# Asking for three weight matrices sooner, and moving the routing's small tables out of two weight cells

## The chip, the cores and the metric

The kernel runs on one core of one Trainium2 chip. The metric is the device time of a whole run in microseconds (us), median of several runs; the profile is of one execution, and its times count from the start of its span.

## The reference

One decoder layer on 256 tokens of width 1024, all in float32. A mixer (three head groups: stick-breaking attention, a gated linear recurrence, cross attention) is normalised by groups, projected and added to x. Then comes the mixture of experts, which is where nearly all bytes are:

```python
scores = sigmoid(t @ w_router)                    # 256 x 64
choice = scores + router_bias
# best 4 of 8 groups of experts by the sum of their two best choices, then top 8 experts in those
_, eidx = top_k(where(emask, choice, -inf), 8)
w = scores at eidx, divided by their sum, times 2.5
for each of 64 experts e (w_gate, w_up: 1024 x 256, w_down: 256 x 1024):
    out += gate[:, e] * ((silu(t @ w_gate) * (t @ w_up)) @ w_down)
out += one shared expert of the same shape, for every token
```

The weights of one expert are 3 MiB, those of all 64 are 192 MiB, and the shared expert has 3 MiB more.

## The kernel before

**Stages.** TensorE (PE) works through a list of units of the mixer (semaphore `unit_ps` counts them), then twelve pieces of the output projection (`projections`, counted by `wo_ps`; pieces 1 to 4 read rows k = 0 to 3 of the matrix `wo`, pieces with k = 4, 5 come as 5, 6, 9, 10, those with k = 6, 7 as 7, 8, 11, 12), the transposes of the normalised x1 into `xn2T`, the router's product (`rt_ps`), the counts, and then 28 groups of experts.

**Groups.** Experts 1 to 6 of the list are fixed (the reference's first six). The other 58 are ranked by how many tokens chose them, and their ids are known only when the vector engine writes `ids` (`ids_dve`). A group holds one, two or four experts side by side in 128 columns; two groups (8 and 15) are halves of the shared expert, which stands in the list as expert 0. For each group PE gathers its tokens, does gate and up with the weights' low half and high half (`gu_ps` goes up after each), the down product (`y_ps`, two steps), and the scatter into four accumulators.

**Cells.** Weights go into 22 cells of 8 KB per partition (1 MiB each) and one more that is used once. A matrix part is "low" or "high" (halves of gate and up) or "down"; each is 1 MiB. From group 8 on "low" and "high" of an expert may come as one load of 2 MiB ("both") into two neighbouring cells, and from group 16 on all three parts as one of 3 MiB ("whole") if three neighbours are free soon enough. A planner at build time (`take`, `last_use`, `held`, `used_at`) walks the list of loads and gives each the cells whose present contents are used up first. Two cells have special places: cell 15 at `o_O + 8 KB` and cell 21 at `o_O + 16 KB`. Before the change the routing's small tensors (`w_rt`, `rbias`, `top8`, `gtop`, `grep`, `score`, `choice` in the first, `cand`, `repl`, `gatew`, `pos_T` in the second) lie in them, so that low 7 (cell 15) waits for `gates_dve`, and cell 21 is held by an entry ("late", None) until `gateT_ps` and `gates_dve`.

**The order of loads.** All weight loads are issued by the sync engine (SP) on one queue, in program order; SP waits in front of a load until its cell is free, and everything behind it waits too. The order of the first ones is written by hand (lines 528 to 564); from line 566 on it is the planner's list: down 0, low 7, low 8, low 9, low 10, high 7, and so on. Down 0 waits for the last step of `split_dve` (the low part of x1, made by the vector engine at L1239) and for `residual_ps`, since it lands on x1. A ranked load also waits for `ids_dve` and reads its expert's id into a register (L571).

Names in the rows: `cell_gu` is a 1 MiB gate/up load, `cell_d` a down load, `cell_two` and `cell_three` those of 2 and 3 MiB. L473 issues them all. L1641 are the projections, L1564 the column sums of `y_sq`, L1676 the router's product, L1734 the gather, L1776 gate and up, L1805 down, L1834 the scatter.

Of the kernel before, what the change touches and what calls it, by code (L numbers as in the profile page):

```python
# [5 lines left out]
def hybrid_decoder_layer(  # L6
# [12 lines left out]
    ACT = mybir.ActivationFunctionType  # L19
    AX = mybir.AxisListType  # L20

    P = 128
    _, SEQ, D = x.shape
    NT = SEQ // P
    KD = D // P
# [3 lines left out]
    NE, GROUPS, DE = w_router.shape[2], 8, w_down_sh.shape[1]  # L29
# [8 lines left out]
    CELLS = 22  # L38
# [15 lines left out]
    for i, kind in enumerate(kinds):  # L54
# [9 lines left out]
        if kind != "fixed":  # L64
            r = {"single": singles, "pair": pairs, "quad": quads}[kind].pop(0)
# [12 lines left out]
    loads, used_at = [], {}  # L78
# [22 lines left out]
    def at(name, offset, shape, dt=F32):  # L101
        return nc.alloc_sbuf_tensor_at(name, shape, dt, offset=offset)
# [23 lines left out]
    neighbours = [(a, b) for a in range(CELLS) for b in range(CELLS) if cell_at[b] == cell_at[a] + 8 * KB]  # L126
    held = dict(zip(first_cells, loads))
    del held[CELLS]
    held[CELLS - 1] = ("late", None)
    used_at["late", None] = (0, 1.5)  # L130
    fills = [1] * (CELLS - 1) + [0, 1]
    cell_of = dict(zip(loads, first_cells))
    landed = {load: (i, 1) for load, i in cell_of.items()}
# [77 lines left out]
    rg_t = r("rg_t", [P, 2, SEQ])  # L211
    rg_u = r("rg_u", [P, 2, SEQ])
    y_sq = at("y_sq", o_R + 16 * KB, [P, KD, SEQ])
    x1_sq = at("x1_sq", o_R + 8 * KB, [P, D])
    xhi = at("xhi", o_R, [P, NT, KD, P], F32R)
    xn2T = at("xn2T", o_R + 16 * KB, [P, KD, SEQ])
    yhi = at("yhi", o_R + 16 * KB, [P, D], F32R)
    ylo = at("ylo", o_R + 20 * KB, [P, D], F32R)

# [26 lines left out]
    rstd_row = at("rstd_row", r.offset + 7 * KB, [P, SEQ])  # L246
    yT = r("yT", [P, KD, SEQ])
    x1 = at("x1", o_O, [P, NT, D])
    rt = Space(o_O + 8 * KB)
    w_rt = rt("w_rt", [P, KD, NE])  # L250
    rbias = rt("rbias", [P, NE])
    top8 = rt("top8", [P, NT, GROUPS, 8])
    gtop = rt("gtop", [P, NT, 8])
    grep = rt("grep", [P, NT, 16])
    rt = Space(o_O + 12 * KB)
    score = rt("score", [P, NT, NE])
    choice = rt("choice", [P, NT, NE])
    rt = Space(o_O + 14 * KB + 6 * KB)
    cand = rt("cand", [P, NT, NE])
    repl = rt("repl", [P, NT, NE])  # L260
    gatew = rt("gatew", [P, NT, NE])
    rt = Space(o_O + 14 * KB + 2 * KB)
    pos_T = rt("pos_T", [NE, SEQ])
    assert rt.offset <= o_O + 14 * KB + 6 * KB
    rt = Space(o_O + 24 * KB)
    e_sg = at("e_sg", rt.offset, [P, DE])
    e_h = at("e_h", rt.offset, [P, KH, P])
    e_hT = rt("e_hT", [P, KH, P])
    S = rt("S", [P, SEQ], F32R)
    gates2 = rt("gates2", [P, NT, NE, 2], F32R)  # L270
    pick0 = rt("pick0", [P, NT, 2 * P], F32R)
    gatesv = rt("gatesv", [P, NT, NV, 2], F32R)
    gslot = rt("gslot", [P, 2])
    ov_gslot = rt("ov_gslot", [P, 1])
    item = rt("item", [P, 4])
# [3 lines left out]
    ident = r("ident", [P, P])  # L279
    ones = r("ones", [P, P])  # L280
    pick = [pick0, at("pick1", r.offset, [P, NT, 2 * P], F32R)]
    wg = r("wg", [P, 2, 2, HD])
    upper = r("upper", [P, P], BF16)
    upper_off = r("upper_off", [P, P], BF16)
# [38 lines left out]
    with ExitStack() as ctx:  # L323
# [151 lines left out]
        def wait_cell(sp, part, e):  # L475

            for held_part, held_e in taken_from[part, e]:
                if held_part == "late":
                    sp.wait_ge(gateT_ps, 1)
                    sp.wait_ge(gates_dve, 1)  # L480
                    continue
                at_group = used_at[held_part, held_e][0]
                if held_part == "down" or held_e in whole:
                    sp.wait_ge(y_ps, 2 * at_group + 2)
                else:
                    sp.wait_ge(gu_ps, 2 * at_group + (1 if held_part == "low" else 2))

        @block.sync
        def _(sp):
# [29 lines left out]
            def load_fixed(part, e):  # L519
                load_cell(sp, part, e, expert(part, e - 1))  # L520

            def load_shared(part):
                if part == "down":
                    load_cell(sp, part, 0, w_down_sh[0].rearrange("(p k) n -> p k n", k=KH))
                else:
                    load_cell(sp, part, 0, w_gu_sh[0, :, PARTS.index(part)])
# [12 lines left out]
            sp.wait_ge(z_ps, SB_HEADS)  # L539
            sp.dma_start(x1[:], x[0].rearrange("(t p) d -> p t d", p=P)).then_inc(x1_loaded, 16)  # L540
            sp.wait_ge(o_ps, SB_HEADS)
            sp.dma_start(w_rt[:], w_router[0].rearrange("(p k) e -> p k e", k=KD)).then_inc(rt_loaded, 16)
            sp.dma_start(rbias[:], router_bias[0].partition_broadcast(P)).then_inc(rb_loaded, 16)
            load_shared("high")
            load_fixed("low", 3)
            load_fixed("high", 3)
# [6 lines left out]
            load_fixed("low", 5)  # L553
            load_fixed("low", 6)
            sp.wait_ge(unit_ps, 33)
            load_fixed("high", 5)
            sp.wait_ge(wo_ps, len(projections))
            load_fixed("high", 6)
            load_fixed("down", 5)
            load_shared("low")  # L560
            sp.wait_ge(ssq_act, 7)
            load_fixed("down", 6)
            sp.wait_ge(rt_ps, NT)
            load_fixed("down", 2)

            for part, e in loads[3 * FIXED + 2:]:
                if e > FIXED and part in ("low", "both", "whole"):
                    sp.wait_ge(ids_dve, 1)
                    if e == min(g.experts[0] for g in groups if e in g.experts):
                        first, chosen = e, []  # L570
                    chosen.append(nc.sync.value_load(ids[0:1, e - FIXED - 1:e - FIXED], min_val=0, max_val=NE - 1))  # L571
                if (part, e) in taken_from:
                    wait_cell(sp, part, e)
                elif cell_of.get((part, e)) == 15:
                    sp.wait_ge(gates_dve, 1)
                else:
                    sp.wait_ge(split_dve, NT + 1)
                    sp.wait_ge(residual_ps, 1)
                if e == 0:
                    load_shared(part)  # L580
                elif e <= FIXED:
                    load_fixed(part, e)
                elif part == "down" and e in groups[-1].experts:
                    i = cell_of[part, e]
                    sp.dma_start(cell_d[i][:, 0:1], ranked("down", chosen[e - first])[:, 0:1]).then_inc(cell_loaded[i], 16)  # L585
                else:
                    load_cell(sp, part, e, ranked(part, chosen[e - first]))
# [111 lines left out]
        def _(act):  # L699
# [167 lines left out]
            for t in range(NT):  # L867
                act.wait_ge(ssq_act, 4 + t)
                if t == 0:
                    act.wait_ge(x1_dve, 8)  # L870
                    nc.scalar.activation(x1_sq[:], x1[:, 0, :], ACT.Square, accum_out=stat[:, 0:1]).then_inc(ssq_act, 1)
                else:
                    for half, col in ((0, 12), (1, 1)):
                        c = slice(half * 512, (half + 1) * 512)
                        act.wait_ge(x1_dve, 11 + half)
                        nc.scalar.activation(x1_sq[:, c], x1[:, 1, c], ACT.Square, accum_out=stat[:, col:col + 1]).then_inc(ssq_act, 1)
                act.wait_ge(xn_dve, 5 + 2 * t)
                nc.scalar.activation(stat[:, 2 + t:3 + t], stat[:, 2 + t:3 + t], ACT.Sqrt).then_inc(std_act, 1)
                if t == 0:
                    high_part(t)  # L880
# [1180 lines left out]
```

## Time and profile before

| | |
|---|---|
| median of 3 runs | 584.82 us |
| the three runs | 584.45, 584.82, 632.85 us |
| span of the profiled execution | 581.9 us |
| median less span | 2.9 us |
| PE busy | 551.5 us, 95% of the span |
| bytes moved by DMA | 227.50 MB, 390 GB/s read over the span |
| weight loads in flight | on one queue, 93.8% of 16 DMA engines' span |

The profile gives no device time of its own for the profiled execution beside the span, so the sums below are made against 581.9 and carried over to the median. A stretch of the DMA's rate well under 420 GB/s is one in which its queue was empty or stalled.

### The profile page before, as it was taken

The numbers are of one execution on the slowest core, as the hardware profiler recorded it, in microseconds if no ns is written. First come the engines' busy times: TensorE is split into PE (matmuls) and PEld (weight loads), VectorE is DVE, ScalarE is ACT, GpSimd is POOL, SyncE is SP. The second block draws the span as 40 slices with busy tenths as digits, with TensorE's granted clock in tenths as the row PEclk, the third lists the DMA queues.
The fourth block names the chain that finished last, engine by engine and source line by source line (L and its number), as shares of the span: only waits on it lengthen the run. The fifth ranks groups of instructions, "written<-read, shape, count | busy, mean of one in ns | idle before, by whom it ended". The sixth has DMA issues, their size and how long they took to land.

```text
span 581.9 us, 8339 instructions
## 1 busy us (share of the span) xinstructions
PE 551.5 (95%) x3164; PEld 307.0 (53%) x3165; DVE 209.2 (36%) x533; ACT 159.5 (27%) x308; POOL 24.2 (4%) x78
## 2 busy tenths in 40 slices
PE   7999999999999999999999989999999899689975
PEld 6988875465444445455455444554554444245332
DVE  2788798684335222220222221212212221220213
ACT  4787367352211222220222221121121122121102
POOL 1006131000000000000000000000000000000000
PEclk9999999999999999999999999999999999898999
DMA  8997459759999999999999999999999999999995
GB/s 315 419 420 302 181 214 410 300 224 367 417 421 419 422 420 420 426 427 425 425 426 426 422 423 434 416 427 430 423 425 434 425 422 426 421 425 427 421 410 200
DMA packets 27496, 227.50 MB, mean 391 GB/s; under 512 B 3264, under 2 KB 3392, under 8 KB 7744
## 3 DMA queue, kind: packets, MB, share of 16 engines
q1 hardware_dynamic: 27168, 226.67, 93.8%
q8 instruction: 26, 0.43, 0.3%
q10 hardware_dynamic: 288, 0.29, 0.1%
q14 instruction: 14, 0.11, 0.0%
HBM read 225.90 MB, written 1.05 MB: 390 GB/s over the span
## 4 chain that ended last, share of the span: by engine, by line
PE 71%; DMA 16%; SPq 8%; DVE 3%; issue 1%; ACT 0%
PE ps L1776 26%; PE ps L1805 11%; DMA cell_two<-in_w_e 10%; PE ps L1734 7%; PE ps L1834 5%; PE ps L1641 5%; SPq L473 4%; PE ps L1537 4%; DMA cell_three<-in_w_e 3%; PE ps L1504 3%; SPq L591 2%; DMA cell_d<-in_w_e 2%; PE ps L1518 2%; SPq L585 1%; PE ps L1796 1%
## 5 line engine op out<-in xcount | busy, mean ns | idle before, releaser
L1776 PE MATMUL ps<-cell_two,xg 128*64 128x512 f32 (+2 forms) x576 | 116.2, 611 | 12.9 <-DMA cell_two<-in_w_e 11.0
L1805 PE MATMUL ps<-cell_d,e_hT 128*64 128x512 f32 (+2 forms) x464 | 89.7, 597 | 2.1 <-DVE e_hT L1396 2.1
L1776 PEld LDWEIGHTS ps<-cell_two,xg 128*64 128x64 f32 (+2 forms) x576 | 37.6, 129 | 89.2 <-issue 89.1
L1776 PE MATMUL ps<-cell_gu,xg 128*64 128x512 f32 (+2 forms) x416 | 78.6, 595 | 1.3 <-DMA cell_gu<-in_w_e 1.2
L1393 DVE TENSOR_TENSOR e_h<-e_sg,ps 128x256 f32<-128x256 f32 x28 | 11.8, 421 | 181.2 <-ACT e_sg L911 181.2
L911 ACT ACTIVATE e_sg<-ps 128x256 f32<-128x256 f32 x28 | 10.7, 384 | 202.9 <-PE ps L1776 202.9
L1461 DVE SCALAR_TENSOR_TENSOR ylo<-ps,gslot,yhi 128x512 fp32r<-128x512 f32 (+1 forms) x53 | 39.2, 740 | 73.8 <-ACT yhi L922 73.8
L1734 PE MATMUL ps<-pick,xhi 128*128 128x256 f32 x224 | 58.4, 300 | 0.3 <-DVE pick L1309 0.3
L922 ACT ACTIVATE yhi<-ps,gslot 128x512 fp32r<-128x512 f32 (+1 forms) x53 | 35.9, 679 | 71.6 <-PE ps L1805 70.2
L1734 PE MATMUL ps<-pick,xlo 128*128 128x256 f32 x224 | 54.3, 281 | 0.0
L1734 PEld LDWEIGHTS ps<-pick,xhi 128*128 128x128 f32 x224 | 42.2, 189 | 19.8 <-issue 19.7
L1776 PEld LDWEIGHTS ps<-cell_gu,xg 128*64 128x64 f32 (+2 forms) x416 | 25.8, 128 | 49.0 <-issue 48.9
L1805 PEld LDWEIGHTS ps<-cell_d,e_hT 128*64 128x64 f32 (+2 forms) x464 | 25.9, 125 | 44.1 <-issue 43.3
L1834 PE MATMUL ps<-yhi,S 128*128 128x512 f32 x102 | 42.2, 414 | 1.8 <-DVE ylo L1461 1.8
L1734 PEld LDWEIGHTS ps<-pick,xlo 128*128 128x128 f32 x224 | 42.4, 189 | 1.0 <-issue 1.0
L1834 PE MATMUL ps<-ylo,S 128*128 128x512 f32 x102 | 40.0, 392 | 0.0
L895 ACT ACTIVATE xg<-ps,vec 128x256 f32<-128x256 f32 x60 | 25.2, 471 | 30.1 <-PE ps L1734 30.0
L1427 DVE TENSOR_TENSOR xg<-ps,vec 128x512 f32<-128x512 f32 x26 | 18.0, 691 | 32.2 <-PE ps L1734 32.2
L1641 PE MATMUL ps<-wo,yT 128*128 128x512 f32 x64 | 29.1, 600 | 0.0
L1776 PE MATMUL ps<-cell_three,xg 128*64 128x512 f32 (+1 forms) x64 | 28.2, 593 | 0.0
L918 ACT CAST S<-ps 128x256 fp32r<-128x256 f32 x26 | 9.7, 372 | 57.5 <-PE ps L1790 57.5
L1390 DVE TENSOR_REDUCE gslot<-ps 64x1 f32<-64x2 f32 (+2 forms) x64 | 10.0, 157 | 39.2 <-ACT S L918 38.0
(342 smaller groups left out, 672.4 us busy)
## 6 DMA issues: line engine op xcount, KB each, us to landing
cell_two<-in_w_e SPq DMA_DIRECT2D x36, 2048.0 KB, 26.4
cell_d<-in_w_e SPq DMA_DIRECT2D x56, 1024.0 KB, 25.7
cell_gu<-in_w_e SPq DMA_DIRECT2D x48, 1024.0 KB, 18.0
cell_three<-in_w_e SPq DMA_DIRECT2D x4, 3072.0 KB, 21.4
wo<-in_w_out SPq DMA_DIRECT2D x1, 4096.0 KB, 12.3
wA<-in_w_qk SPq DMA_DIRECT2D x7, 512.0 KB, 11.6
wR<-in_w_rest SPq DMA_DIRECT2D x3, 1024.0 KB, 28.0
wV<-in_w_v SPq DMA_DIRECT2D x1, 2048.0 KB, 18.7
```

Source lines behind the costliest of these rows:

```text
L473: sp.dma_start({"down": cell_d, "both": cell_two, "whole": cell_three}.get(part, cell_gu)[i][:], src).then_inc(cell_loaded[i], 16)
L895: nc.scalar.mul(rows_of(c, slice(k, k + 1), slice(0, 2)).squeeze(1), ps[:, Y[step % 2], k % 2 * 2 * P:(k % 2 + 1) * 2 * P].rearrange("p (g ...
L922: nc.scalar.mul(yhi[:, c], o, gslot[:, g.routed % 2:g.routed % 2 + 1]).then_inc(yhi_act, 1)
L1427: nc.vector.tensor_tensor(rows_of(c, slice(2 * step, 2 * step + 2), slice(0, 2)), ps[:, Y[1], :].rearrange("p (k g s) -> p k g s", k=2, g= ...
L1461: nc.vector.scalar_tensor_tensor(ylo[:, c], o, gslot[:, g.routed % 2:g.routed % 2 + 1], yhi[:, c].bitcast(F32), ALU.mult, ALU.subtract).th ...
L1504: last = mm(b[:, 0:SEQ], part[:, k, :], a[:, k, :], start=k == 0 and m == 0, stop=k == KD - 1 and m == 2)
L1537: last = mm(b, a[:, k, c:c + P], w[:, k, :], start=k == 0 and m == 0, stop=k == KD - 1 and m == 2)
L1641: last = mm(ps[:, ACC[2 * t + half], :], yT[:, k, t * P:(t + 1) * P], wo[:, k, half * 512:(half + 1) * 512], start=k == chunks[0], stop=k ...
L1734: last = mm(o, part[:, t, k, :], pick[c % 2][:, t, :], start=i == 0, stop=i == 3)
L1776: last = mm(ps[side * w:(side + 1) * w, U, :], rows(k, slice(side * w, (side + 1) * w)), weight[:, k - k0, :], start=k == 0, stop=k == KD - 1)
L1805: last = mm(ps[side * w:(side + 1) * w, Y[half], :], e_hT[:, kk, side * w:(side + 1) * w], n[:, kk, half * 512:(half + 1) * 512], start=kk ...
L1834: last = mm(ps[:, ACC[2 * t + half], :], to_token[:, t * P:(t + 1) * P], y[:, half * 512:(half + 1) * 512], start=False, stop=sem is not N ...
```

## The change

Three things are done. (1) The hand-written order of loads: high 6, down 5, low 0, down 6 and down 2 each get a condition of their own, the first that frees their bytes, and the order becomes down 6, low 0, down 2, high 6, down 5. To free them, `x1_sq` moves from `o_R + 8 KB` to `o_R`, and `xn2T` from `o_R + 16 KB` to `o_A`. (2) The router's matrix `w_rt` (256 KB) and `rbias` (32 KB, one row copied to 128 partitions) are loaded into other places, so their loads move from behind `o_ps` to behind `unit_ps` 33, ahead of high 5. (3) The routing's tensors leave cells 15 and 21: the holder of cell 21 becomes ("free", None), with no wait, and the wait of low 7 for `gates_dve` goes. The planner then gives low 8 the cell 21, and every later load gets cells by the same rule from that start.

```diff
-    held[CELLS - 1] = ("late", None)
-    used_at["late", None] = (0, 1.5)
+    held[CELLS - 1] = ("free", None)
+    used_at["free", None] = (-1, 0)
...
-    x1_sq = at("x1_sq", o_R + 8 * KB, [P, D])
+    x1_sq = at("x1_sq", o_R, [P, NT, D])
     xhi = at("xhi", o_R, [P, NT, KD, P], F32R)
-    xn2T = at("xn2T", o_R + 16 * KB, [P, KD, SEQ])
+    xn2T = at("xn2T", o_A, [P, KD, SEQ])
...
+    w_rt = at("w_rt", o_V + 12 * KB, [P, KD, NE])
...
+    rbias = at("rbias", r.offset, [P, NE])
+    pos_T = at("pos_T", r.offset, [NE, SEQ])
...
-                if held_part == "late":
-                    sp.wait_ge(gateT_ps, 1)
-                    sp.wait_ge(gates_dve, 1)
+                if held_part == "free":
                     continue
...
             sp.wait_ge(o_ps, SB_HEADS)
-            sp.dma_start(w_rt[:], w_router[0].rearrange("(p k) e -> p k e", k=KD)).then_inc(rt_loaded, 16)
-            sp.dma_start(rbias[:], router_bias[0].partition_broadcast(P)).then_inc(rb_loaded, 16)
             load_shared("high")
...
             sp.wait_ge(unit_ps, 33)
+            sp.dma_start(w_rt[:], w_router[0].rearrange("(p k) e -> p k e", k=KD)).then_inc(rt_loaded, 16)
+            sp.dma_start(rbias[:], router_bias[0].partition_broadcast(P)).then_inc(rb_loaded, 16)
             load_fixed("high", 5)
+            sp.wait_ge(yrg_dve, 2)
+            load_fixed("down", 6)
+            sp.wait_ge(wo_ps, 4)
+            load_shared("low")
+            sp.wait_ge(unit_ps, 35)
+            load_fixed("down", 2)
+            sp.wait_ge(wo_ps, 10)
+            load_fixed("high", 6)
             sp.wait_ge(wo_ps, len(projections))
-            load_fixed("high", 6)
             load_fixed("down", 5)
-            load_shared("low")
-            sp.wait_ge(ssq_act, 7)
-            load_fixed("down", 6)
-            sp.wait_ge(rt_ps, NT)
-            load_fixed("down", 2)
...
                 if (part, e) in taken_from:
                     wait_cell(sp, part, e)
-                elif cell_of.get((part, e)) == 15:
-                    sp.wait_ge(gates_dve, 1)
-                else:
+                elif e == 0:
                     sp.wait_ge(split_dve, NT + 1)
                     sp.wait_ge(residual_ps, 1)
```

The planner's list changes in this way (worked out from its rule): loads keep their order up to expert 35; low 8 is freed by nothing instead of by low 1, low 10 by low 2 instead of high 1, high 8 by high 2 instead of the "late" holder. Later releases move by at most three phases of a group, mostly to an earlier one. Experts 36, 42 and 48, which came as one load of 3 MiB, come as 2 MiB and 1 MiB; expert 50 stays whole.

## Rows read from the trace of the kernel before

**Rows 1.** The page: GB/s moved in 40 equal slices of the span (14.55 us each).

```profile
GB/s 315 419 420 302 181 214 410 300 224 367 417 421 419 422 420 420 426 427 425 425 426 426 422 423 434 416 427 430 423 425 434 425 422 426 421 425 427 421 410 200
```

**Rows 2.** Windows: busy us of each engine (instructions), PE clock, DMA share, GB/s.

```profile
83.00:88.50 5.50, 5.50 (x30) 2.76 (x31) 3.85 (x8) 5.40 (x12) 1.52 (x3) 1.00 0.54 147
88.50:106.00 17.50, 17.50 (x80) 9.37 (x76) 16.23 (x39) 10.50 (x28) 1.79 (x3) 1.00 1.01 423
...
112.50:121.60 9.10, 9.10 (x30) 4.46 (x29) 5.96 (x11) 3.17 (x6) 0.00 (x0) 1.00 0.02 7
121.60:126.00 4.40, 4.40 (x42) 4.40 (x41) 2.95 (x12) 2.66 (x7) 0.00 (x0) 1.00 0.76 266
126.00:132.70 6.70, 6.28 (x30) 3.42 (x29) 6.24 (x38) 2.83 (x4) 0.00 (x0) 1.00 1.01 423
132.70:136.70 4.00, 3.90 (x25) 2.51 (x26) 3.41 (x16) 1.68 (x4) 0.00 (x0) 1.00 0.96 401
136.70:144.40 7.70, 7.70 (x43) 3.68 (x40) 1.17 (x5) 1.68 (x4) 0.00 (x0) 1.00 0.90 328
144.40:151.20 6.80, 6.42 (x42) 4.09 (x42) 3.55 (x13) 2.70 (x7) 0.00 (x0) 1.00 1.01 426
151.20:154.60 3.40, 3.40 (x18) 1.38 (x16) 0.75 (x1) 0.53 (x1) 0.00 (x0) 1.00 1.01 419
154.60:164.60 10.00, 9.73 (x50) 4.66 (x50) 1.91 (x5) 1.60 (x4) 0.00 (x0) 1.00 1.00 414
...
500.00:565.00 65.00, 53.16 (x316) 24.18 (x318) 11.11 (x28) 8.76 (x17) 0.00 (x0) 0.95 1.01 421
```

**Rows 3.** SP's issues in order of time: start us, us, line, load, how many.

```profile
106.00 0.33 SPq L473 DMA_DIRECT2D cell_gu<-in_w_e  x1
121.65 0.33 SPq L473 DMA_DIRECT2D cell_gu<-in_w_e  x1
122.02 0.43 SPq L473 DMA_DIRECT2D cell_d<-in_w_e  x1
122.50 0.43 SPq L473 DMA_DIRECT2D cell_gu<-in_w_gu_sh  x1
123.25 3.08 SPq L473 DMA_DIRECT2D cell_d<-in_w_e  x2
132.73 0.33 SPq L473 DMA_DIRECT2D cell_d<-in_w_down_sh  x1
136.68 3.67 SPq L473 DMA_DIRECT2D cell_gu<-in_w_e  x3
144.38 1.85 SPq L473 DMA_DIRECT2D cell_gu<-in_w_e  x3
151.17 3.77 SPq L473 DMA_DIRECT2D cell_gu<-in_w_e  x2
155.12 3.77 SPq L473 DMA_DIRECT2D cell_d<-in_w_e  x3
```

**Rows 4.** Waits of SP from 132 to 137 us: in total, times, longest.

```profile
SPq L473 <- DVE xlo L1239: 3.2, 1, 3.2
SPq L571 <- DVE ids L1331: 2.0, 1, 2.0
SPq L473 <- DVE gates L1338: 0.7, 1, 0.7
```

**Rows 5.** DMA issues by tensor: KB each, us from issue to landing.

```profile
w_rt<-in_w_router SPq DMA_DIRECT2D x1, 256.0 KB, 2.7
...
rbias<-in_router_bias SPq DMA_DIRECT2D x1, 32.0 KB, 5.5
```

**Rows 6.** The vector engine and PE in order of time, ahead of the router.

```profile
120.78 0.07 DVE L1283 MEMSET grp<- 128x8 f32 x1
...
121.90 1.00 PE L1676 MATMUL ps<-w_rt,xn2T 128*128 128x64 f32 x8
```

**Rows 7.** Waits of PE in the whole span.

```profile
PE ps L1776 <- DMA cell_two<-in_w_e: 11.0, 4, 4.8
```

More of the change, by code:

```diff
@@ L248, in hybrid_decoder_layer @@
     x1 = at("x1", o_O, [P, NT, D])
[L249 to L264, printed above, removed]
+    w_rt = at("w_rt", o_V + 12 * KB, [P, KD, NE])
     rt = Space(o_O + 24 * KB)
+    score = at("score", rt.offset, [P, NT, NE])
+    choice = at("choice", rt.offset + NT * NE * 4, [P, NT, NE])
     e_sg = at("e_sg", rt.offset, [P, DE])
@@ L268, in hybrid_decoder_layer @@
     e_hT = rt("e_hT", [P, KH, P])
+    top8 = at("top8", rt.offset, [P, NT, GROUPS, 8])
+    gatew = at("gatew", rt.offset, [P, NT, NE])
+    cand = at("cand", rt.offset + NT * NE * 4, [P, NT, NE])
     S = rt("S", [P, SEQ], F32R)
@@ L271, in hybrid_decoder_layer @@
     pick0 = rt("pick0", [P, NT, 2 * P], F32R)
+    route_space = Space(rt.offset)
+    repl = route_space("repl", [P, NT, NE])
+    gtop = route_space("gtop", [P, NT, 8])
+    grep = route_space("grep", [P, NT, 16])
     gatesv = rt("gatesv", [P, NT, NV, 2], F32R)
+    assert route_space.offset <= rt.offset
     gslot = rt("gslot", [P, 2])
@@ L870, in _ @@
                     act.wait_ge(x1_dve, 8)
-                    nc.scalar.activation(x1_sq[:], x1[:, 0, :], ACT.Square, accum_out=stat[:, 0:1]).then_inc(ssq_act, 1)
+                    nc.scalar.activation(x1_sq[:, 0, :], x1[:, 0, :], ACT.Square, accum_out=stat[:, 0:1]).then_inc(ssq_act, 1)
                 else:
@@ L875, in _ @@
                         act.wait_ge(x1_dve, 11 + half)
-                        nc.scalar.activation(x1_sq[:, c], x1[:, 1, c], ACT.Square, accum_out=stat[:, col:col + 1]).then_inc(ssq_act, 1)
+                        nc.scalar.activation(x1_sq[:, 1, c], x1[:, 1, c], ACT.Square, accum_out=stat[:, col:col + 1]).then_inc(ssq_act, 1)
                 act.wait_ge(xn_dve, 5 + 2 * t)
```

## The prediction

> **What bounds the kernel now.** I read the page's line of GB/s first. From slice 10 (131 us) to slice 38 the DMA moves 410 to 434 GB/s without a break [rows 1]. PE is busy too, but it waits for weights: 11.0 us in four waits for 2 MiB loads [rows 7], and between 500 and 565 us it works 53.16 of 65 us while the DMA works all of it at 421 GB/s [rows 2]. So from the first ranked experts on, the end is "when did the queue become full for good, plus the bytes left over 424 GB/s", and one MiB (1.05 MB) is 2.47 us. Only DMA time that is idle before that point, and that the change really fills with bytes that would else have been moved after it, shortens the run.
>
> The windows show where it idles or crawls: 147 GB/s from 83.0 to 88.5, 7 GB/s from 112.5 to 121.6, 266 from 121.6 to 126.0, 328 from 136.7 to 144.4, and 414 or more in every window after [rows 2]. The 9.1 us hole at 112.5 is the one that the change aims at. SP's issues show what stands around it: high 5 at 106.00, then nothing until 121.65, then five matrices, down 0 at 132.73, and the ranked ones from 136.68 in threes [rows 3].
>
> **When the queue is full for good.** Issues less bytes moved give what is still queued. Between 112.5 (empty) and 154.6 SP issued 1+1+1+2+1+3+3+1 = 13 loads of 1.05 MB = 13.63 MB [rows 3] (the second of the pair at 151.17 goes out at the end of that row, at 154.6). Moved: 0.06 + 1.17 + 2.83 + 1.60 + 2.53 + 2.90 + 1.42 = 12.51 MB [rows 2]. So 1.12 MB or 2.6 us are queued at 154.6. Ten us later, with four more issued (4.19 MB) and 4.14 moved, it is 1.17 MB or 2.8 us, and the rate never drops after. Two things follow: nothing after 144 us is idle, and the DMA could run ahead by at most about 2.6 us there before it waits for PE to free cells. 2.6 us is the ceiling of this change, whatever it fills earlier.
>
> **Part 1, three matrices sooner.** Down 6, low 0 and down 2 go out behind high 5 instead of from 122.5 on; high 6 and down 5 follow when their piece of `wo` is read, the last at the old 121.65 at the latest. The queue has 1.52 MB at 106 (issued since 83: 9 loads and the two tables, 9.73 MB; moved 5.5 x 147 and 17.5 x 423 GB/s, 8.21 MB [rows 2]), so the hole fills: five matrices need 12.4 us, and they are landed by 121.65 + 1.6 + 2.5 = 125.8 at the latest, where 1.6 us is what a start on an empty queue cost at 121.6 (4.4 us at 266 instead of 424 [rows 2]). But what is next does not move. Down 0 waits for the vector engine's `xlo` until 132.7, and the first ranked load stands behind it and waits for the ids until 2.0 us later [rows 3, 4]. No other cell is free then. The idle time of 112.5 to 121.6 therefore comes back as idle time from 125.8 to 132.7; the hole is moved, not filled.
>
> What is left of part 1 is how soon the queue is through with static matrices. Before: at 132.7 five loads issued (5.24 MB) less 4.06 moved, 1.18 MB, plus down 0: 2.23 MB, done at 138.0. After: down 0 alone, on an empty queue: 132.73 + 1.64 + 2.47 = 136.8. Low 7 was issued at 136.68 and cannot flow at full rate before 136.68 + 1.64 = 138.3, so before it was its issue that bound, just. This holds after too.
>
> **Part 3, cells 15 and 21 free.** The wait for `gates` is 0.7 us long [rows 4]; without it low 7 goes out at 136.0, flows from 137.6 (after down 0's 136.8), so the stream of ranked weights begins 0.7 us sooner. Low 8 no longer waits for group 0's low half: 137.1 instead of about 138.6 (a ranked load with its id costs 1.1 us of SP; so do the ones at 168 us, and this is an estimate from three issues in 3.67 us, one wait among them [rows 3]). Low 10 goes out near 139.7 instead of 144.38. So four MiB instead of three are available between 136 and 144.4, in which the DMA moved only 2.53 MB of the 3.26 that 424 GB/s gives [rows 2]: 1.7 us lost although about 2 MB were queued. I can't tell from the trace whether this came from the thin queue (16 engines that do not run dry together) or from the first reads of far-away weights. Bounds: 0 to 1.7 us of it come back. I take 0.3, nearer to 0, because at 151.2 to 164.6 the queue is as thin (1.1 MB) and the rate is 414 to 419.
>
> The new plan of cells costs nothing that I can find: its releases are the same phase or one to three sooner for nearly all loads. The worst place is expert 41's, two phases later, some 7 us by the pace of one group in 14 or 15 us; it costs nothing while 3 MB are queued, and the page's steady 420 GB/s and more [rows 1] shows a queue that was never near empty there. The 3 MiB loads of experts 36, 42 and 48 become 2 + 1 MiB. The slice with one such load at its best is at 434 GB/s against 424 around it [rows 1]; if all 9.4 MB lost that, it is 9.4/0.424 - 9.4/0.434 = 0.5 us. Bounds 0 to 0.5, I take 0: 1 MiB loads alone ran at 426 at 144.4 [rows 2]. This is where a rule speaks against the change: the Trainium skill, "DMA: Bandwidth & Descriptors", section Bandwidth, has a lone transfer of 1 MB at 341 GB/s and one of 16 MB at 425, and advises large ones. Where the queue is never empty the trace does not agree (426 GB/s with 1 MiB each). By the page's figures three 1 MiB loads would cost 3 x 0.6 = 1.8 us, an estimate, and the sum would be 1 us slower than before.
>
> **Part 2, the small tables.** They leave 83.0 and land behind high 5's turn. Issued at 106.0, behind at most 1.5 MB (3.6 us) and with their own 2.7 and 5.5 us [rows 5], `rbias` is there by 115.1; the vector engine asks for it at 120.8, ahead of the small L1283, and PE needs `w_rt` at 121.9 [rows 6]. That is 5.7 us of cover for the one and more for the other. The slow stretch 83 to 88.5 (0.81 MB where 2.33 could go) gets shorter by their 0.8 us of SP and by what `rbias` with its 128 rows of 256 bytes held up: at most the 3.6 us that it lost. That too is given back as idle time before 132.7, so worth 0 at the end. If the stall comes with `rbias` to 106, it delays static matrices by the same 3.6 us, into the 6.9 us of idle ahead of 132.7: also 0.
>
> **The sum.** Against the span: 581.9 - 0.7 - 0.3 = 580.9. With the 2.9 us around it: 584.8 - 1.0 = 583.8 us.
>
> **The rivals.**
> 1. The moved hole pays more. If the crawl at 136.7 to 144.4 was a thin queue, 1.7 + 0.7 = 2.4 us come back, just under the ceiling of 2.6: 582.4. For it: the rate recovers at 144.4 when three more loads are issued. Against: as thin a queue at 154.6 runs at full rate.
> 2. It does not do what it says: the three matrices land sooner, nothing used them sooner, and the earlier low 7 and low 8 meet the same crawl: 584.8. For it: PE starts group 0 with its matrices long landed, and neither the router nor the ids come sooner.
> 3. Slower, by the packets: the gain of 0.7 is there or not, and the split of the three large loads costs 0.5 by rows (the page's rule says 1.8): 584.6 to 585.3 and, by the page, 586. It decides if smaller loads lower the rate of a full queue at all, which 426 GB/s speaks against.
> 4. Slower, by the tables: `rbias` and `w_rt` queue behind the weights. Place: the vector engine's wait ahead of the router and PE's at 121.9. Price: 2.47 us for each MiB above the point where it decides, which is (120.8 - 106.0 - 5.5)/2.47 = 3.8 MiB in front of them; I count 1.4. To cost 2% (11.7 us) it would take 8.5 MiB, which is all that SP issued since 83. Only if the 83 to 88.5 crawl were something that grows could this come: 590.
> 5. Much faster: the ranked stream would have to begin 12 us sooner, and the ids forbid it.
>
> **How the numbers follow.** Forecast (583.4 to 584.4) 0.5; rival 1 with 582.4 0.2; rival 2 with 584.8 0.15; rival 3 0.1; rival 4 0.03; the rest, 0.02, is for what I overlooked on the faster side. A run's median itself is uncertain by some 0.4 us (584.45 and 584.82), and a full queue's rate by 0.3% of 430 us, 1.3 us. So the range goes from 582.4 - 1.3 = 581.1 to 584.8 + 1.3 = 586.1. 2% (11.7 us) is about what a measurement of this kernel can tell from no change: faster by more 0.02, slower by more 0.03, within 0.95.
>
> **What would show it.** In the profile after: GB/s near 420 up to about 120 to 124 us, a new hole of some 7 us that ends at 133, and PE's times up to 136 unchanged; `w_rt` and `rbias` issued near 106 and no wait of PE for `w_rt`; low 7 issued at 136.0 and low 8 at 137.1; the windows 136.7 to 144.4 show whether the crawl stays at 328; at 154.6 the queue holds 0.4 MB less; from 200 us on all windows at 424, and the last landing one us sooner. I am wrong if the crawl goes away altogether, if the DMA shows idle time near 154 or 164 (the lead was lost against PE), if a later window drops under 420, or if the router waits. If the ids come sooner, I have missed a dependence.

## The result

| | before | changed |
|---|---|---|
| median | 583.62 us (22 runs, 582.57 to 632.85) | 584.71 us (22 runs, 583.13 to 586.76) |
| ratio to before | | 1.0019, 95% interval 1.0011 to 1.0027 |
| span of the profiled execution | 581.9 us | 582.3 us |

The prediction was 583.8 us with 584.8 for no change, a ratio of 0.998. The time lies in its range and within 2%, but the gain of 1.0 us did not come: the changed kernel measured 0.2% slower. (The 632.85 us is one disturbed run and in no ratio.) The base of the sum was high as well: the first three runs of before had a median of 584.82 us, all 22 of them have 583.62. So the ratio is what counts, not the distance of 584.71 from 583.8.

**The page after**, GB/s in 40 slices (14.56 us each), which answers to [rows 1]:

```profile
GB/s 318 419 420 298 186 271 424 345 241 314 383 382 423 423 420 421 429 424 423 425 425 424 429 419 426 427 424 426 426 422 427 433 420 427 422 425 424 423 409 184
```

The slice of 131 to 146 us is at 314 where before had 367, and the two of 146 to 175 us stand at 383 and 382, where before had 417 and 421. The windows show it closer, with the bounds of [rows 2]:

```profile
83.00:88.50 5.50, 5.50 (x32) 2.87 (x32) 3.28 (x6) 5.41 (x12) 1.58 (x3) 1.00 0.93 338
...
106.00:112.50 6.50, 6.50 (x19) 3.14 (x19) 3.16 (x8) 1.82 (x6) 0.73 (x1) 1.00 0.80 243
112.50:121.60 9.10, 9.10 (x33) 4.71 (x32) 5.91 (x11) 3.22 (x6) 0.00 (x0) 1.00 1.00 407
121.60:126.00 4.40, 4.40 (x37) 4.08 (x37) 3.02 (x16) 3.18 (x8) 0.00 (x0) 1.00 0.85 270
126.00:132.70 6.70, 6.27 (x33) 3.69 (x32) 6.21 (x36) 2.70 (x5) 0.00 (x0) 1.00 0.10 44
132.70:136.70 4.00, 3.90 (x24) 2.17 (x25) 2.93 (x13) 1.25 (x4) 0.00 (x0) 1.00 0.95 287
136.70:144.40 7.70, 7.70 (x46) 4.08 (x42) 1.18 (x5) 2.06 (x6) 0.00 (x0) 1.00 0.94 383
144.40:151.20 6.80, 6.42 (x41) 3.80 (x41) 3.55 (x13) 2.84 (x6) 0.00 (x0) 1.00 1.02 423
151.20:154.60 3.40, 3.40 (x20) 1.35 (x18) 0.75 (x1) 0.00 (x0) 0.00 (x0) 1.00 0.88 323
154.60:164.60 10.00, 9.73 (x52) 4.55 (x52) 1.92 (x6) 2.13 (x4) 0.00 (x0) 1.00 1.00 397
164.60:170.00 5.40, 5.40 (x49) 3.18 (x42) 2.04 (x6) 0.84 (x2) 0.00 (x0) 1.00 0.96 322
170.00:200.00 30.00, 30.00 (x207) 14.45 (x210) 13.03 (x46) 5.94 (x12) 0.00 (x0) 1.00 1.01 421
```

The last column times the length of the window is bytes. The hole has moved from 112.5 (7 GB/s) to 126.0 (44 GB/s), the crawl of 136.7 to 144.4 is at 383 instead of 328, and at 144.4 us this profile has moved 20.16 MB since 83 us, before's 18.93: 1.23 MB or 2.9 us ahead. Then come the rows to dwell on: 323 GB/s at 151.2, 397 at 154.6, 322 at 164.6. Before had 419, 414 and 422 there. At 154.6 the lead is 0.88 MB, at 164.6 it is 0.71, at 170 it is 0.17 MB (0.4 us). The lead was there and is lost in 20 us. From 170 us on both profiles read alike.

The two profiles are shifted against each other by 0.56 us (next paragraph), which makes this lead look some 0.2 MB too large. e11, a copy of before in the third group below, is not shifted: it issues down 0 at 132.17 us, the changed kernel at 132.16. Against e11 the changed kernel is ahead by 0.50 MB at 136.7, by 1.14 MB (2.7 us) at 144.4, by 0.81 at 154.6, by 0.55 at 164.6 and by 0.00 at 170.

SP's issues, which answer to [rows 3] and [rows 5] (this profile runs 0.56 us earlier than before's from PE's first wait on, so 0.56 comes off before's times):

```profile
105.43 0.33 SPq L549 DMA_DIRECT2D w_rt<-in_w_router  x1
105.80 0.43 SPq L550 DMA_DIRECT2D rbias<-in_router_bias  x1
106.28 0.43 SPq L470 DMA_DIRECT2D cell_gu<-in_w_e  x1
...
132.16 0.33 SPq L470 DMA_DIRECT2D cell_d<-in_w_down_sh  x1
135.48 0.35 SPq L470 DMA_DIRECT2D cell_gu<-in_w_e  x1
136.61 0.34 SPq L470 DMA_DIRECT2D cell_gu<-in_w_e  x1
...
150.62 0.33 SPq L470 DMA_DIRECT2D cell_gu<-in_w_e  x1
154.05 0.33 SPq L470 DMA_DIRECT2D cell_gu<-in_w_e  x1
```

Low 7 and low 8 go out at 135.48 and 136.61, on before's scale 136.04 and 137.17. But the loads at 150.62 and 154.05 go out when they did before (151.17 and about 154.6 less 0.56).

Waits of SP from 131 to 137 us (for [rows 4]): the one for `gates` is gone, the others are the same to the tenth.

```profile
SPq L470 <- DVE xlo L1234: 3.2, 1, 3.2
SPq L568 <- DVE ids L1326: 2.0, 1, 2.0
```

The router (for [rows 6]) starts as before, and the tables' loads (DMA view, 105 to 121 us) take 4.6 and 5.7 us; PE has no wait for `w_rt`:

```profile
121.33 1.00 PE L1671 MATMUL ps<-w_rt,xn2T 128*128 128x64 f32 x8
```

```profile
w_rt<-in_w_router SPq DMA_DIRECT2D x1, 256.0 KB, 4.6
rbias<-in_router_bias SPq DMA_DIRECT2D x1, 32.0 KB, 5.7
```

The slow stretch moved with the tables: 83.0 to 88.5 us is at 338 GB/s instead of 147, and 106.0 to 112.5 is at 243, where e4, which has the tables back at 83 us, has 421. That loss lies ahead of the hole, so it costs nothing at the end.

### The profile page after: what moved, and what is told of

Same layout as the page of the kernel before. It is cut to its first block, busy times and chain, and to the rows that moved or that the text cites. A ratio compares the mean times of both kernels' runs of the same rounds, so it can differ in the third digit from the quotient of the medians.

```text
span 582.3 us, 8347 instructions
## 1 busy us (share of the span) xinstructions
PE 552.1 (95%) x3164; PEld 307.3 (53%) x3165; DVE 209.3 (36%) x533; ACT 159.5 (27%) x308; POOL 24.2 (4%) x78
## 3 DMA queue, kind: packets, MB, share of 16 engines
HBM read 225.90 MB, written 1.05 MB: 390 GB/s over the span
## 4 chain that ended last, share of the span: by engine, by line
PE 71%; DMA 21%; SPq 4%; DVE 3%; issue 1%; ACT 0%
PE ps L1771 27%; DMA cell_two<-in_w_e 14%; PE ps L1800 10%; PE ps L1729 7%; PE ps L1829 5%; PE ps L1636 5%; DMA cell_three<-in_w_e 4%; PE ps L1532 4%; PE ps L1499 3%; SPq L586 2%; DMA cell_d<-in_w_e 2%; PE ps L1513 2%; SPq L580 1%; PE ps L1791 1%; PE ps L1521 1%
## 5 line engine op out<-in xcount | busy, mean ns | idle before, releaser
L1771 PE MATMUL ps<-cell_two,xg 128*64 128x512 f32 (+2 forms) x624 | 123.5, 611 | 13.1 <-DMA cell_two<-in_w_e 11.4
L1800 PE MATMUL ps<-cell_d,e_hT 128*64 128x512 f32 (+2 forms) x488 | 93.4, 597 | 2.7 <-DVE e_hT L1391 2.7
L1771 PEld LDWEIGHTS ps<-cell_two,xg 128*64 128x64 f32 (+2 forms) x624 | 41.0, 131 | 93.4 <-issue 93.4
L1800 PEld LDWEIGHTS ps<-cell_d,e_hT 128*64 128x64 f32 (+2 forms) x488 | 27.4, 127 | 46.2 <-issue 45.4
L1829 PEld LDWEIGHTS ps<-yhi,S 128*128 128x128 f32 x102 | 19.2, 188 | 7.0 <-issue 3.8
```

The lines of the kernel that those rows point to most:

```text
L1771: last = mm(ps[side * w:(side + 1) * w, U, :], rows(k, slice(side * w, (side + 1) * w)), weight[:, k - k0, :], start=k == 0, stop=k == KD - 1)
L1800: last = mm(ps[side * w:(side + 1) * w, Y[half], :], e_hT[:, kk, side * w:(side + 1) * w], n[:, kk, half * 512:(half + 1) * 512], start=kk ...
L1829: last = mm(ps[:, ACC[2 * t + half], :], to_token[:, t * P:(t + 1) * P], y[:, half * 512:(half + 1) * 512], start=False, stop=sem is not N ...
```

## The experiments

Runs of one group shared a chip and the runs of before. Two theories stood at the start. Theory 1: the lead in bytes is real and is lost at 150 to 170 us, because cells come free with PE's groups. Theory 2: the lead is kept, and something of the change's own (the new plan with the split 3 MiB loads, the tables' stall) takes it back. In the expectations of e1 to e6 theory 1 is called the dry-queue or slowest-ring theory, and theory 2 the load-size theory (the split loads) and the tables theory.

**First group: the change taken apart** (before: 583.93 us, 35 runs).

*e1: the kernel before with part 1 alone* (the new order of static loads, `x1_sq` and `xn2T` moved).

```diff
-            sp.wait_ge(wo_ps, len(projections))
-            load_fixed("high", 6)
...
+            sp.wait_ge(yrg_dve, 2)
+            load_fixed("down", 6)
+            sp.wait_ge(wo_ps, 4)
+            load_shared("low")
...
```

> Part 1 alone: down 6, low 0, down 2 (and high 6, down 5) are asked for early, the tables and cells 15 and 21 stay as before. Dry-queue theory (every start on an empty or nearly empty queue costs 1 to 2 us on some of the 16 DMA engines, and a lead over PE is lost where cells come free too slowly, 151 to 170 us): the hole moves to about 125 to 132 us, down 0 then starts on an empty queue, the lead at 144 us is under 1 us and is gone by 170; ratio to before 1.000 to 1.001. Load-size theory (the three 3 MiB loads that became 2 + 1 MiB are the loss): the plan is the old one, ratio 1.000. Tables theory (rbias in a thin queue at 106 us is the loss): ratio 1.000.

Measured: 584.03 us, ratio 0.9995 [0.998, 1.001].

*e2: the changed kernel with the static matrices in the old order*, so tables and cells alone (the reverse of the diff above, in the changed kernel).

> Parts 2 and 3 alone: the tables are moved and cells 15 and 21 are free, but the five static matrices go out in the old order at the old conditions. Dry-queue theory: no hole ahead of 132 us, so the queue still holds about 1 MiB there and the ranked loads start in step; low 7 and low 8 come 0.7 and 1.5 us sooner; the gain is 0 to 0.7 us, ratio 0.999 to 1.000. Load-size theory: ratio 1.002, all of the loss. Tables theory: ratio about 1.002, all of the loss.

Measured: 584.63 us, 1.0011 [0.9995, 1.0027].

*e3: the changed kernel with the planner started as before* (the old plan, no wait at cell 21).

```diff
-    held[CELLS - 1] = ("free", None)
-    used_at["free", None] = (-1, 0)
+    held[CELLS - 1] = ("late", None)
+    used_at["late", None] = (0, 1.5)
...
-                if held_part == "free":
+                if held_part == "late":
                     continue
```

> The changed kernel with the planner started as before, so that all cells and load sizes (four loads of 3 MiB) are those of before; only the waits of low 7 for the gates and of high 8 are gone. Load-size theory: ratio 1.000 or a little under. Dry-queue theory: the hole at 126 to 132 us stays, ratio 1.001 to 1.002. Tables theory: 1.002.

Measured: 584.83 us, 1.0012 [0.9998, 1.0025].

*e4: the changed kernel with the two tables loaded behind `o_ps` as before* (at `o_O + 8 KB` and `+ 10 KB`).

```diff
             sp.wait_ge(o_ps, SB_HEADS)
+            sp.dma_start(w_rt[:], ...).then_inc(rt_loaded, 16)
+            sp.dma_start(rbias[:], ...).then_inc(rb_loaded, 16)
             load_shared("high")
```

> The changed kernel with the loads of w_rt and rbias back behind o_ps at 83 us (into cell 15, which is free until the ids are known). Tables theory: the slow stretch at 106 to 112 us goes and with it the loss, ratio 1.000. Dry-queue and load-size theories: ratio stays at 1.002.

Measured: 584.11 us, 1.0009 [0.9995, 1.0023].

What follows from the four: all their intervals overlap, and no part can be named as the one that costs or gives. (The gain of up to 0.7 us that the dry-queue theory allowed e2 was not seen: e2's median is 0.7 us over before's, with 0.3 us of gain still inside its interval.) The traces say more than the times. MB moved since 83 us, each summed from the windows with the bounds above:

| | 136.7 | 144.4 | 154.6 | 164.6 | 170 |
|---|---|---|---|---|---|
| e1 part 1 alone | 17.11 | 20.00 | 23.91 | 27.73 | 29.99 |
| e2 tables and cells alone | 16.63 | 19.60 | 23.88 | 27.95 | 29.82 |
| e3 old plan | 17.20 | 19.83 | 23.79 | 27.51 | 29.77 |
| e4 tables back | 17.12 | 19.99 | 24.02 | 27.71 | 29.77 |

They differ by 0.57 MB at 136.7 and by 0.22 at 170. Part 1 by itself has nearly the whole lead at 144.4 (0.98 MB over e11) and loses it just so; so theory 2 in its forms "the new plan" and "the tables" isn't needed for the loss.

**Second group: how sure is the 0.19%?** (before: 583.49 us, 35 runs).

*e5: the kernel before with a comment line added*, the same program.

> The kernel before once more, for a second trace of it. All theories: ratio 1.000 within 0.0015. Slowest-ring theory (each load is split over 16 DMA rings, lands when the slowest has its share, and a ring that ran dry stays behind for good): low 7 lands about 8 us after its issue, and the first and the last ring end 5 to 6 us apart at the end of the run (DMA share under 1 from about 568 us on).

Measured: 584.41 us, 1.0013 [1.0003, 1.0022]. A copy of before measures slower than before.

*e6: the changed kernel again.*

> The changed kernel once more, for a second trace. Slowest-ring theory: low 7 lands 5 us after its issue, 3 to 4 us sooner than before; of that lead nothing is left from about 195 us on, lost where the queue runs thin at 151 to 170 us; ratio 1.001 to 1.002. If instead the loss at 151 to 170 was chance in one trace, DMA moves 419 GB/s or more at 151 to 155 and 164 to 170 us here.

Measured: 584.2 us, 1.0011 [0.9999, 1.0023], which is 0.2 us less than the copy of before. So the 0.19% of the first measurement is hardly larger than what one and the same program shows when it is measured again. As the slowest-ring theory expected, low 7 lands 8.2 us after its issue in e5 and 5.2 us in e6; and e6 has the slow windows again (323 GB/s at 151.2, 379 at 164.6), so they are no chance of one trace.

*e7: the changed kernel, low 7 and low 8 held as before.*

```diff
+                if part == "low" and e == FIXED + 1:
+                    sp.wait_ge(gates_dve, 1)
+                if part == "low" and e == FIXED + 2:
+                    sp.wait_ge(gu_ps, 1)
```

> The changed kernel, but low 7 waits for the gates and low 8 for group 0's low half again, as before; same cells, same places of the tables. If the earlier ranked loads only build a lead that is lost at 151 to 170 us (slowest-ring theory), the landings from about 195 us on and the time are those of the changed kernel, ratio 1.001 to 1.002, or a little better if fewer rings run dry. If the earlier release of the two cells itself is worth its 0.7 us, this one is 0.7 us slower than the changed kernel, ratio 1.003.

Measured: 584.38 us, 1.0022 [1.0008, 1.0036]. It is at 19.80 MB at 144.4 and 30.08 at 170, no fewer than the changed kernel's 29.84: taking back the 0.7 us of earlier issue took nothing from the bytes at 170. Its time against e6 is 0.2 us, not to be told from none; the 0.7 us that the earlier release might be worth is not excluded by the times, only by the bytes.

*e8: the kernel before without any 3 MiB load* (`WHOLE_FROM` 16 becomes 99).

> The kernel before with no 3 MiB loads at all: all four are split into 2 + 1 MiB (the change splits three). Load-size theory as the cause of the loss: ratio 1.002 or more. By the bytes moved in the traces so far, three splits cost 0.17 us between 350 and 500 us, so four cost 0.2 us and the ratio is 1.000 to 1.0005.

Measured: 583.88 us, 1.0005 [0.999, 1.0021]: splitting all of them costs nothing that can be told.

**Third group: the same hold in both kernels, each beside its copy** (before: 584.2 us, 35 runs).

```diff
+                if part == "low" and e == FIXED + 1:
+                    sp.wait_ge(gu_ps, 1)
                 if (part, e) in taken_from:
                     wait_cell(sp, part, e)
```

*e9: the kernel before with it. e11: before once more, with another comment.*

> The kernel before, but the first ranked load (low 7) also waits until PE has done the low half of group 0 (gu_ps 1), some 1.7 us later (about 138.4 instead of 136.7 us); everything behind it on SP's queue moves too. Every theory: before has no lead to lose (its queue holds about 1 MiB at 151 and 154 us and its rate stays over 410), so it ends 1.2 to 1.7 us later than an identical copy of before in the same rounds. If it ends within 0.5 us of the copy, then neither kernel is set by when the ranked stream starts, and my account of the end is wrong altogether.

> The same program as before with another comment at its end, the yardstick for the hold in before and a second measure of what resubmitting does. If the shared runs of before and a copy are alike, the ratio is 1.000 within 0.001; if a copy measures slower by itself, as the first copy did (1.0013), it is 1.0005 to 1.002.

Measured: e9 584.17 us, 1.0004 [0.9992, 1.0016]; e11 584.21 us, 1.0006 [0.9995, 1.0018]. The hold moved low 7 from 136.13 to 138.15 us and cost nothing. No theory expected that: all had it 1.2 to 1.7 us later. Windows of e11, then of e9:

```profile
136.70:144.40 7.70, 7.70 (x45) 4.07 (x42) 1.18 (x5) 2.05 (x6) 0.00 (x0) 1.00 0.89 300
138.00:140.00 2.00, 2.00 (x17) 1.80 (x17) 0.00 (x0) 1.32 (x4) 0.00 (x0) 1.00 0.84 291
140.00:144.00 4.00, 4.00 (x21) 1.48 (x21) 1.18 (x5) 0.36 (x1) 0.00 (x0) 1.00 0.86 272
...
151.20:154.60 3.40, 3.40 (x20) 1.35 (x18) 0.75 (x1) 0.00 (x0) 0.00 (x0) 1.00 1.00 417
154.60:164.60 10.00, 9.73 (x52) 4.56 (x52) 1.91 (x5) 2.13 (x4) 0.00 (x0) 1.00 1.01 423
164.60:170.00 5.40, 5.40 (x49) 3.16 (x42) 2.03 (x6) 0.84 (x2) 0.00 (x0) 1.00 1.02 423
```

```profile
136.70:144.40 7.70, 7.70 (x44) 3.95 (x41) 1.17 (x5) 1.93 (x5) 0.00 (x0) 1.00 0.82 311
138.00:140.00 2.00, 2.00 (x16) 1.87 (x16) 0.00 (x0) 1.20 (x3) 0.00 (x0) 1.00 0.51 115
140.00:144.00 4.00, 4.00 (x21) 1.41 (x21) 1.17 (x5) 0.48 (x2) 0.00 (x0) 1.00 0.94 385
```

Over 136.7 to 144.4 both move the same. The copy crawls at 291 and 272 GB/s while its DMA engines are busy 84 and 86% of the time; the held one stands nearly still (115 GB/s) and then goes at 385. The crawl would have wasted the 2 us of the hold in any case.

*e10: the changed kernel with the hold. e12: the changed kernel once more.*

> The changed kernel with the same wait ahead of low 7 (gu_ps 1), about 2.0 to 2.5 us later (138.0 instead of 135.5 to 136 us). Theory 1 (the lead of some 2.9 us at 144 us is lost at 150 to 170 us, because the cells come free with PE's groups and the queue runs thin): the hold takes a lead that is lost anyway, so it ends 0 to 0.5 us later than an identical copy of the changed kernel, the lead in bytes at 144 us is under 1.2 us, and the windows 151.2 to 154.6 and 164.6 to 170 are at 380 GB/s or more instead of 323 and under. Theory 2 (the lead is kept, and something else in the changed kernel, such as the split 3 MiB loads or the plan of cells, takes it back evenly): the hold costs what it costs in before, 1.2 to 2 us more.

> The changed kernel again, the yardstick for the hold in it. Theory 1 (the change makes no difference that can be told): within 0.1% of the copy of before in the same rounds, either way. Rival (the changed kernel is really slower by 0.1 to 0.2%): 0.6 to 1.1 us over the copy of before.

Measured: e10 583.96 us, 1.0005 [0.9994, 1.0015]; e12 584.38 us, 1.001 [0.9999, 1.0021]. Windows of e12, then of e10:

```profile
136.70:144.40 7.70, 7.70 (x45) 3.91 (x42) 1.17 (x5) 1.84 (x5) 0.00 (x0) 1.00 0.97 376
...
151.20:154.60 3.40, 3.40 (x18) 1.38 (x16) 0.75 (x1) 0.20 (x1) 0.00 (x0) 1.00 0.87 328
154.60:164.60 10.00, 9.73 (x52) 4.61 (x52) 1.91 (x5) 1.93 (x4) 0.00 (x0) 1.00 0.98 385
164.60:170.00 5.40, 5.40 (x51) 2.94 (x40) 1.80 (x6) 1.04 (x3) 0.00 (x0) 1.00 0.94 358
```

```profile
151.20:154.60 3.40, 3.40 (x18) 1.38 (x16) 0.60 (x1) 0.00 (x0) 0.00 (x0) 1.00 1.00 417
154.60:164.60 10.00, 9.73 (x54) 4.54 (x54) 2.06 (x6) 2.13 (x4) 0.00 (x0) 1.00 1.01 419
164.60:170.00 5.40, 5.40 (x50) 3.23 (x42) 2.04 (x6) 0.84 (x2) 0.00 (x0) 1.00 1.02 422
```

The hold takes the changed kernel's lead, and with it the slow rows go. In MB since 83 us, summed as above:

| | 144.4 | 154.6 | 164.6 | 170 |
|---|---|---|---|---|
| e11 before | 19.02 | 23.32 | 27.55 | 29.84 |
| e9 before, held | 19.04 | 23.30 | 27.56 | 29.81 |
| e12 changed | 20.03 | 24.04 | 27.89 | 29.82 |
| e10 changed, held | 19.17 | 23.49 | 27.68 | 29.96 |

e12 is 1.01 MB (2.4 us) ahead of e11 at 144.4, and 0.02 behind at 170. e10 has no lead that can be told from none: its 19.17 and 29.96 MB lie among those of the copies of before (e5 has 19.29 and 29.96). Its time is 0.4 us under e12's, where theory 1 had 0 to 0.5 us over it; what speaks for theory 1 is that the lead and the slow windows go together. e10 reads the same weights at full rate, so which weights are read is not what makes these windows slow. SP's issues say why a lead goes, of e11 and then of e12:

```profile
150.62 0.33 SPq L473 DMA_DIRECT2D cell_gu<-in_w_e  x1
154.05 0.33 SPq L473 DMA_DIRECT2D cell_gu<-in_w_e  x1
...
164.02 0.33 SPq L473 DMA_DIRECT2D cell_d<-in_w_e  x1
```

```profile
150.85 0.33 SPq L470 DMA_DIRECT2D cell_gu<-in_w_e  x1
154.28 0.33 SPq L470 DMA_DIRECT2D cell_gu<-in_w_e  x1
...
164.24 0.33 SPq L470 DMA_DIRECT2D cell_d<-in_w_e  x1
```

Both kernels issue at the same times (e12's profile is 0.22 us late throughout), since each of these loads waits for PE to be done with a cell. Of e11, waits of SP from 140 to 172 us:

```profile
SPq L473 <- PE ps L1805: 10.3, 2, 5.5
SPq L473 <- PE ps L1776: 10.2, 4, 3.4
```

A DMA that is ahead finds no more loads there, only less in its queue. Issues less bytes moved, counted from a moment at which the queue was empty, give what is queued just before the issues near 150.7, 154.2 and 164.1 us: 1.66, 1.30 and 1.26 MiB in e11, 1.60, 1.21 and 1.19 in e10, 0.61, 0.51 and 0.87 in e12, and 0.59, 0.49 and 0.76 in the first profile of the changed kernel.

The rate does not fall at once. It falls when the load that joined the thin queue gets its turn, 1 us and more behind its issue. Windows from 1.0 to 3.4 us behind these issues (150.62, 154.05 and 164.01 us), of the changed kernel, and the first of them in e11:

```profile
151.62:154.02 2.40, 2.40 (x14) 0.95 (x12) 0.33 (x1) 0.00 (x0) 0.00 (x0) 1.00 0.86 300
155.05:157.45 2.40, 2.40 (x13) 0.82 (x10) 0.00 (x0) 0.10 (x1) 0.00 (x0) 1.00 0.96 352
165.01:167.41 2.40, 2.40 (x25) 0.59 (x17) 1.14 (x5) 0.00 (x0) 0.00 (x0) 1.00 1.01 287
```

```profile
151.62:154.02 2.40, 2.40 (x14) 0.96 (x12) 0.35 (x1) 0.00 (x0) 0.00 (x0) 1.00 1.02 423
```

The same two numbers, taken at the three issues of all 16 profiles (before, changed and e1 to e14), go together:

| queued at the issue, MiB | how many | GB/s, 1.0 to 3.4 us later |
|---|---|---|
| 0.49 to 0.93 | 16 | 287 to 365 |
| 0.99 to 1.05 | 7 | 365 to 413 |
| 1.11 to 1.66 | 19 | 389 to 434 |
| 3.55 and more | 6 | 403 to 430 |

So at these places about 1 MiB has to be queued when the next load joins; with less, the DMA is slow for some 3 us.

**Fourth group: does the end follow the bytes at all?** (before: 583.16 us, 7 runs.) After e9 this had to be asked. *e13: the kernel before, held until both halves of group 0 are done. e14: the changed kernel with the same.*

```diff
+                if part == "low" and e == FIXED + 1:
+                    sp.wait_ge(gu_ps, 2)
```

> The kernel before, with low 7 held until PE has done both halves of group 0 (gu_ps 2), to about 144.2 us: 8 us later than the copy's 136.1, 6 us later than in the first hold, which cost nothing. Nothing flows from about 139 to 144, so at 144 us the deficit against the copy (45.2 MB) is about 1.5 MB or 3.6 us, and a restart on an empty queue costs 0.5 to 1.6 us more. Theory A (from about 150 us on the end is the bytes left over a constant rate, and only what exceeds the crawl of 136.7 to 144.4 us is a delay): it ends 3.5 to 5.2 us later than before, 587.7 to 589.4 us, and all windows from 151 us on are like the copy's. Theory B (the end does not follow the DMA's bytes, PE or something else sets it): less than 1.5 us later.

> The changed kernel with the same long hold of low 7 (to about 143.6 us). Theory A: its lead is gone before the ranked stream starts, both held kernels begin it at the same time on an empty queue, so it ends within 0.7 us of the long hold in before. If the changed plan of cells or the split 3 MiB loads cost more than 0.7 us, it ends later than that one by as much.

Measured: e13 589.87 us, 1.0112 [1.009, 1.0133]; e14 590.14 us, 1.0111 [1.0082, 1.0141]. Windows of e13:

```profile
136.70:144.40 7.70, 7.70 (x46) 4.13 (x43) 1.18 (x5) 2.12 (x6) 0.00 (x0) 1.00 0.14 60
144.40:151.20 6.80, 6.42 (x40) 3.80 (x41) 3.60 (x14) 2.80 (x6) 0.00 (x0) 1.00 0.95 358
...
164.60:170.00 5.40, 5.40 (x50) 3.23 (x42) 2.04 (x6) 0.84 (x2) 0.00 (x0) 1.00 1.02 425
```

Since 83 us it has 27.47 MB at 170, e11 29.84: 2.37 MB or 5.6 us behind. At 500 us the two sums are 167.57 and 170.04, 2.47 MB or 5.8 us. The time went up by 6.7 us against before's runs in the same rounds and by 5.7 against e11, which ran on another chip. The end does follow the bytes once they are short, so the account was not wrong altogether, as e9's expectation feared; what e9 shows is that the crawl hides a hold of 2 us. The expectation was 3.5 to 5.2 us. The deficit in bytes came out above it: 1.91 MB (4.5 us) at 144.4, where the copy had gone on moving, and another 1.1 us by 151.2 for the restart on an empty queue. e14 is 0.3 us over e13 with the other plan of cells: within what can't be told.

## Why the prediction was wrong

**What held.** The hole was moved, not filled, and ends at 133. Down 0, low 7 and low 8 went out when the text said, within 0.1 us. The tables were covered; their stall came along to 106 us and cost nothing, as the text allowed. The steady windows from 200 to 565 us stayed at 421 to 426. (One slip of reading: the full slices of [rows 1] begin at 146 us, not at 131; the slice of 131 has 367. The windows, on which the sum rests, were read rightly.) Two landings were set too soon. The five static matrices were to be there by 125.8 us at the latest; the last one lands at 128.25, 128.8 on before's scale, still ahead of 132.7. And in the kernel before down 0 was to be done at 138.0; it lands at 140.18.

**The crawl was undersized.** The text gave it 0.3 us back of 0 to 1.7, and so a lead of 1.0 us at 144. In e12 against e11, it is 0.43 MB (1.0 us) at 136.7, and the crawl gives another 7.7 x (376 - 300) = 0.59 MB (1.4 us): 2.4 us in all. The first profile of the changed kernel has 2.7 us at that place. That is near rival 1's 0.7 + 1.7 = 2.4 us at 144 us, and wrong at the end. The text left open whether the crawl came from a thin queue or from first reads of far-away weights. The changed kernel reads the same weights at 376 to 383 GB/s, so the second is not it; the crawl, like the slow windows later, follows a load that joined a thin queue (low 7 in before, at 0.66 MiB). Why the changed kernel's low 7, at 0.28 MiB and 3 us after an empty queue, did not bring the same crawl is not shown.

**The step that failed** is the ceiling: "2.6 us is the ceiling of this change", since 1.12 MB are queued at 154.6 "and the rate never drops after". It took the whole queue for room in front. The arithmetic was right; what it left out is that about 1 MiB has to be queued here for the full rate (0.93 MiB and less gave 365 GB/s at most, 1.11 and more gave 389 at least). Before and its copies have 1.02 to 1.30 MiB at 154 us and 1.11 to 1.26 at 164. So before stood nearly at the ceiling already: 0 to 0.3 MiB, under 1 us, not 2.6. With 2.4 us of lead e12 has 328, 385 and 358 GB/s in the three windows and pays all of it back by 170. The text's own row, 414 to 419 GB/s with 1.1 MB queued, told that this much is enough and nothing of what less would do. The prediction named the symptom in its last part ("if the DMA shows idle time near 154 or 164 (the lead was lost against PE)"), and gave it no chance and no price.

**Its sum also began in the wrong place.** From low 7's issue it concludes: "so the stream of ranked weights begins 0.7 us sooner". That took an issue time for a time at the end. In e9 the issue is 2.0 us later and the end does not move. Of the two holds tried in before only e13's, 7.6 us, counted, with 5.7 to 6.7 us.

**The terms of the sum** therefore measured as follows: 0.7 us for the sooner issue and 0.3 us from the crawl were a lead of 2.4 to 2.7 us at 144 us, and 0.0 of it was left at 170. The 2.9 us around the span was no constant: for the changed kernel's profiled execution it is 1.7 us (584.03 less 582.3).

**Rivals.** The outcome is rival 2 (no gain), with 584.8, but for another cause: it had the crawl unchanged, and the lead did come and was lost later. Rival 3 (packets): the Trainium skill, "DMA: Bandwidth & Descriptors", section Bandwidth, has 341 GB/s for 1 MB and 425 for 16 MB, from which the text estimated 1.8 us for the three split loads. e8, which splits all four in the kernel before, shows 0.4 us against before's runs, with an interval from -0.6 to +1.2 us, and is under the copy of before in the same rounds (583.88, 584.41). The measurement doesn't agree with the 1.8; the 0.5 us by rows is not excluded.

**The 0.2% slower.** Against before's shared runs the changed kernel was at 1.0019, 1.0011 and 1.001, and copies of before at 1.0013 and 1.0006. In the rounds where both copies ran it was 584.20 against 584.41 and 584.38 against 584.21. The mean of 23 runs of each is 584.42 and 584.21: 0.2 us more, plus or minus 0.5. So no difference is shown; a loss of up to 0.7 us is not excluded, and nor is a gain of 0.3. Why copies of before measure above before's shared runs stays open.

## What to carry to other kernels

Filling an idle stretch of DMA is worth only as much as the DMA may then run ahead, and that room is what is queued less what the queue needs to run at full rate, read at the thinnest place after it. Here it was at most 0.3 MiB, with 1.02 to 1.30 queued and about 1 needed. Look at when the loads behind are issued: where each waits for the consumer to free a buffer, as at 150 to 164 us here, an earlier start gives a thinner queue and no earlier load. To learn whether a start matters, delay it: a hold of 2 us that cost nothing (e9) made it unlikely at once that 0.7 us less would bring anything, and the bytes moved at a later point (170 us here) tell more than times with a spread of 0.5 us.

## What was not expected of the hardware

A thin queue is slow before it is empty, and with a delay: in the changed kernel the DMA is slow from 152 us on, when one more MiB has joined the 0.59 of 150.6. In e12 the window 151.2 to 154.6 has the DMA engines busy 87% of the time at 328 GB/s, 377 for a fully busy one, where e11 has 417 at 100%: part of the loss is engines without work and part is slower work. In the crawl (e11, 138 to 144 us, 84 and 86% busy, 291 and 272 GB/s) slower work was more than half of the loss, although 0.9 to 2.5 MiB were queued. Loads that started on an empty queue did better (e9, 385 GB/s from 140), so the 1 MiB is no rule for that case. What slows the packets there was not tried and stays open.

The 16 DMA engines end out of step. In the window 565 to 575 us of the changed kernel they are busy 72%:

```profile
565.00:575.00 10.00, 6.99 (x66) 2.30 (x66) 1.62 (x7) 1.33 (x3) 0.00 (x0) 1.00 0.72 270
```

Put together by their starts and ends, since the profile does not name the engine of a packet, e12's packets give a first engine that is done at 568.6 and a last one at 574.5 us. The last weight load lands 10.4 us after its issue in before (574.8) and 11.9 us in its copy e5 (575.7), so some of the spread between runs may be this; that it is was not shown.
